# A transformer kernel on one core: down products of the last feed-forward with the activations stationary and 512 weight columns moving

## What is computed

```python
h2 = rms_norm(x, g_mlp)
x = x + jnp.square(jax.nn.relu(h2 @ w_up)) @ w_down      # w_up: 2048 x 8192, w_down: 8192 x 2048
```

## Time and profile before

| | |
|---|---|
| median of 3 runs | 2577.26 us (2576.41 to 2577.57) |
| time of the profiled execution | 2577.26 us |
| its span in the profile | 2575.6 us |
| mean granted TensorE clock | 0.999 of 2.4 GHz |
| TensorE busy | 2543.1 us, 99% |
| VectorE, ScalarE busy | 69%, 50% |
| DMA | 463.63 MB, 180 GB/s on average |

### The profile page before, as it was taken

One profiled execution on the slowest core, in us unless ns is written; L12 is line 12 of the kernel. 1 busy time (PEld: TensorE's weight loads), 2 busy tenths in 40 slices (PEclk: granted clock), 3 DMA queues, 4 the chain that ended last, 5 costly groups with the idle time before them and its releaser, 6 DMA issues.

```text
span 2575.6 us, 44260 instructions
## 1 busy us (share of the span) xinstructions
PE 2543.1 (99%) x14648; PEld 2240.0 (87%) x14648; DVE 1782.5 (69%) x2958; ACT 1288.6 (50%) x2372; POOL 255.7 (10%) x298
## 2 busy tenths in 40 slices
PE   7999999999999999999999999999999999999999
PEld 6888888888888888889999988888888888888888
DVE  6787789866886788675555566667575665665664
ACT  6656555444444444556555554555454444444443
POOL 0000114311330233100000000001100000000000
PEclk9999999999999999999999999999999999999999
DMA  6454435655556555545555545556465555555554
GB/s 229 163 168 159 164 131 196 193 185 193 184 167 206 187 187 180 193 141 188 175 173 177 162 153 185 184 184 214 153 212 186 187 182 190 186 186 188 182 190 137
DMA packets 163928, 463.63 MB, mean 180 GB/s; under 512 B 18106, under 2 KB 37470, under 8 KB 163806
## 3 DMA queue, kind: packets, MB, share of 16 engines
q1 hardware_dynamic: 163134, 459.91, 54.2%
q0 software_dynamic: 672, 2.11, 0.3%
HBM read 459.81 MB, written 2.14 MB: 179 GB/s over the span
## 4 chain that ended last, share of the span: by engine, by line
PE 82%; DVE 9%; ACT 4%; issue 3%; DMA 1%; POOL 0%; DVEq 0%; SPq 0%; ACTq 0%; POOLq 0%
PE G L712 72%; PE SB L712 9%; DVE wlo L1421 3%; ACT y L1214 1%; PE MB L712 1%; ACT whi L1129 1%; DVE wlo L1414 1%; DVE y L1629 1%; DMA x<-in_xT 0%; ACT y L1221 0%; PE SB L1059 0%; DVE og L1712 0%; ACT whi L1120 0%; DVE y L1809 0%; ACT aS L1292 0%
## 5 line engine op out<-in xcount | busy, mean ns | idle before, releaser
L712 PE MATMUL G<-hS,whi 128*128 128x512 f32 x3712 | 1299.7, 398 | 16.6 <-DVE wlo L1421 14.9
L712 PE MATMUL G<-hS,wlo 128*128 128x256 f32 x3680 | 996.5, 281 | 0.9 <-DVE hS L1863 0.9
L1421 DVE TENSOR_TENSOR wlo<-raw,whi 128x1024 fp32r<-128x1024 f32 (+3 forms) x790 | 902.5, 1182 | 97.8 <-ACT whi L1129 83.1
L712 PEld LDWEIGHTS G<-hS,whi 128*128 128x128 f32 x3712 | 685.3, 188 | 169.1 <-DVE wlo L1421 14.0
L1129 ACT ACTIVATE whi<-raw 128x1024 fp32r<-128x1024 f32 (+3 forms) x790 | 752.9, 998 | 79.6 <-DMA raw<-in_mix 31.1
L712 PEld LDWEIGHTS G<-hS,wlo 128*128 128x128 f32 x3680 | 696.8, 189 | 21.5 <-DVE hS L1863 1.3
L712 PE MATMUL G<-aS,whi 128*128 128x512 f32 (+1 forms) x1952 | 677.2, 398 | 0.8 <-DVE og L1523 0.7
L1192 ACT ACTIVATE tmp<-G 128x256 f32<-128x256 f32 x370 | 141.2, 382 | 879.2 <-PE G L712 879.2
L712 PE MATMUL G<-aS,wlo 128*128 128x256 f32 x1928 | 519.2, 281 | 0.0
L712 PEld LDWEIGHTS G<-aS,whi 128*128 128x128 f32 x1952 | 356.9, 188 | 77.9 <-DVE og L1523 1.0
L712 PEld LDWEIGHTS G<-aS,wlo 128*128 128x128 f32 x1928 | 364.4, 189 | 13.4 <-DVE aS L1716 0.3
(11 more groups left out here) (187 smaller groups left out, 1900.6 us busy)
## 6 DMA issues: line engine op xcount, KB each, us to landing
raw<-in_up SPq DMA_DIRECT2D x304, 512.0 KB, 4.6
raw<-in_dn SPq DMA_DIRECT2D x160, 512.0 KB, 4.5
raw<-in_in SPq DMA_DIRECT2D x192, 256.0 KB, 3.3
raw<-in_in SPq DMA_DIRECT2D x64, 512.0 KB, 4.6
raw<-in_out SPq DMA_DIRECT2D x64, 512.0 KB, 4.5
raw<-in_dn SPq DMA_DIRECT2D x64, 448.0 KB, 3.9
raw<-in_mix SPq DMA_DIRECT2D x64, 384.0 KB, 3.1
raw<-in_mix SPq DMA_DIRECT2D x64, 320.0 KB, 3.3
```

Of the source, the lines that this page charges most:

```text
L712: return pe.matmul(o, w, m, start=start, stop=stop, skip_group_check=False)
L1421: dve.tensor_tensor(wlo[:, slot, a * P:b * P], raw[:, h0 % RAW_SLOTS, 0:(b - a) * P], whi[:, slot, a * P:b * P].bitcast(F32), ALU.subtract ...
```

## The change

All products of `dn2_0`, `dn2_1`, `dn2_2`, and those of the first three iterations of `dn2_3`, are computed in groups of four output tiles (512 features) at once. For each of the 16 blocks of the depth, and each half of 128 tokens, the 128 x 128 activations are stationary and 512 weight columns move: high x high, high x low (`wlo`), low x high, all three summed in one bank. The result has tokens on the partitions. VectorE takes the two banks of a group into `y` (copies them in `dn2_0`, adds afterwards), so that `y` holds the sum over the chunks. At the end it is turned back with 32 PE transposes into the bank `MB` and added to `x`: the last four tiles' sum over three chunks during `up2_3`, the others during `dn2_3`. The last four tiles of `dn2_3` are computed as before. Units hold 4 x 4 blocks in place of 16 blocks of one tile, so a load takes two rows of 2 KB per partition in place of one of 4 KB, and the splits write in another order. On TensorE, ScalarE and VectorE the `dn2` stages are written out in place of the hardware loop; SP writes out `dn2_3` alone. Left out below: the declarations of two semaphores (`back_mm`, `back_added`), the view `yT` of `y`, those loops, the index of `tmp_done`, and empty lines.

```diff
@@ -64,6 +64,7 @@
 W_SLOTS = 4
 UNIT = 16
 AHEAD = 3
+TOKENS = ("dn2_0", "dn2_1", "dn2_2", "dn2_3")
 WIDE = {"up1_0": 4, "up2_0": 3}
 TOGETHER = 11
@@ -145,6 +146,8 @@
         self.bank0 = (prev.bank0 + prev.nm * (1 if prev.nm % 2 and prev.iters == 1 else 0)) % 2 if prev else 0
         self.half = (blocks + 1) // 2
         self.pieces = 3 if name == "in2" else 2
+        self.copied = (prev.copied + (prev.iters * prev.nm if prev.name in TOKENS else 0)) if prev else 0
         self.pbase = prev.pbase + prev.iters * prev.units * prev.pieces if prev else 0
         self.rbase = prev.rbase + (0 if prev.name == "in2" else 2 * prev.iters * prev.units) if prev else 0
@@ -156,6 +159,10 @@
     def g(self, it, p):
         return it * self.nm + (self.gbase + p)
+    def t(self, it, p):
+        return self.g(it, p) - self.copied - (3 * self.nm if self.name == TOKENS[-1] else 0)
     def u(self, it, k):
         return it * self.units + (self.ubase + k)
@@ -283,6 +290,19 @@
             return (G, (SB[2], SB[3]))[g % 2][h]
+        def by_tokens(st, it):
+            return st.name in TOKENS and (st.name != TOKENS[-1] or it < 3)
+        def token_banks(it):
+            return (SB[2], SB[3]) if it % 2 == 0 else (SB[0], SB[4])
+        def group_weights(tensor, slot, half):
+            w = tensor[:, slot, :].rearrange("p (k m n) -> p k m n", k=4, m=4)
+            return w[:, :, 2 * half:2 * half + 2, :]
         def in2_scores(g):
             return SB[0] if g % 2 == 0 else SB[4]
@@ -602,8 +629,13 @@
                     if not (isinstance(it, int) and h < RAW_SLOTS):
                         sp.wait_ge(lo_done, h - (RAW_SLOTS - 1))
+                    src = dram[st.name]
+                    if by_tokens(st, it if isinstance(it, int) else 0):
+                        rows = src[bass.ds(it * 4 + 2 * half, 2)][:, :, 4 * k * P:4 * (k + 1) * P]
+                        sp.dma_start(raw[:, slot, 0:(b - a) * P].rearrange("p (r c) -> p r c", r=2),
+                                     rows.rearrange("r p c -> p r c")).then_inc(landed[slot], 16)
+                        continue
                     row = it * st.units + k
-                    src = dram[st.name]
                     src = src[row] if isinstance(row, int) else src[bass.ds(row, 1)].rearrange("a p c -> (a p) c")
                     sp.dma_start(raw[:, slot, 0:(b - a) * P], src[:, a * P:b * P]).then_inc(landed[slot], 16)
@@ -746,7 +778,57 @@
                             one.then_inc(unit_used, 1)
+            def token_group(st, it):
+                banks = token_banks(it)
+                if it >= 2:
+                    pe.wait_ge(ev_done, st.g(it - 2, 3) + 1)
+                for kk in range(KT):
+                    k, within = divmod(kk, 4)
+                    slot = (st.ubase + k) % W_SLOTS
+                    if within == 0:
+                        pe.wait_ge(lo_done, st.piece(it, k, 1) + 1)
+                    if it == 0:
+                        pe.wait_ge(a_ready, A_BASE["up" + st.name[2:]] + kk + 1)
+                    if st.name == TOKENS[-1] and it and kk in (6, 12):
+                        turn_back(it - 1, kk // 12)
+                    h_w, l_w = (w[:, slot, within * 4 * P:(within + 1) * 4 * P] for w in (whi, wlo))
+                    for half in range(2):
+                        bank = banks[half][:, :]
+                        x_h = hS[:, kk, half * P:(half + 1) * P]
+                        x_l = hS[:, kk, T + half * P:T + (half + 1) * P]
+                        one = mm(bank, x_h, h_w, kk == 0, False)
+                        mm(bank, x_h, l_w, False, False)
+                        end = mm(bank, x_l, h_w, False, kk == KT - 1)
+                        if half == 0 and within == 0:
+                            one.then_inc(unit_used, 1)
+                end.then_inc(mt_done, 4)
+            def turn_back(it, pair):
+                pe.wait_ge(ev_done, ST[TOKENS[-1] if it < 3 else TOKENS[-2]].g(it, 3) + 1)
+                if it == 3 and pair:
+                    pe.wait_ge(back_added, 1)
+                elif it < 3:
+                    pe.wait_ge(back_added, 2)
+                    if it or pair:
+                        pe.wait_ge(x_done, 4 * it + 2 * pair)
+                for m in range(2):
+                    for half in range(2):
+                        at = (it * 4 + 2 * pair + m) * P
+                        end = pe.transpose(MB[:, m * T + half * P:m * T + (half + 1) * P], yT[:, half, at:at + P], ident)
+                end.then_inc(back_mm, 1)
             def mtile(st, it, p, last):
+                if by_tokens(st, it):
+                    if p == 0:
+                        token_group(st, it)
+                    return
                 if is_wide(st, it) and p < WIDE[st.name]:
                     if p == 0:
                         wide_start(st)
@@ -780,6 +862,12 @@
                 if st.name == "out2" and isinstance(it, int) and it == 0 and p < 2:
                     f = ST["out2"].g(0, 0) - 2
+                if st.prev and st.prev.name in TOKENS and isinstance(it, int) and it == 0 and p < 2:
+                    f = st.prev.g(0, 0)
+                if st.name == TOKENS[-1] and p < 2:
+                    f = st.g(0, 0)
                 if is_wide(st, it):
                     f = st.g(0, 0)
@@ -797,6 +885,10 @@
                 spreads = st.name in NORM_IN and isinstance(it, int) and it == 0 and p == (3 if st.wide else 2)
                 for kk in range(a, b):
+                    if st.prev and st.prev.name == TOKENS[-2] and first and (p, kk) in ((1, 4), (2, 4)):
+                        turn_back(3, p - 1)
+                    if st.name == TOKENS[-1] and p == 0 and kk in (6, 12):
+                        turn_back(2, kk // 12)
                     if st.name == "pre" and p == 2 and kk == 8:
                         norm_sums(NORM_IN["pre"])
                     if st.name == "up1_0" and isinstance(it, int) and it == 1 and (p, kk) in ((0, 6), (0, 13)):
@@ -847,6 +939,9 @@
                 high = accumulator(st, it, p)[:, 0:T]
                 pe.wait_ge(ev_done, g - 1)
+                if st.name == last2:
+                    pe.wait_ge(x_done, 12)
                 def at(kk):
                     k, within = divmod(st.start[p] + kk, st.blocks)
@@ -1418,6 +1520,11 @@
                     h0 = st.rbase + 2 * k + half
                     a, b = (0, st.half) if half == 0 else (st.half, st.blocks)
                     dve.wait_ge(hi_done, st.piece(it, k, half) + 1)
+                    if by_tokens(st, it):
+                        dve.tensor_tensor(group_weights(wlo, slot, half),
+                                          raw[:, h0 % RAW_SLOTS, :].rearrange("p (m k n) -> p k m n", m=2, k=4),
+                                          group_weights(whi, slot, half).bitcast(F32), ALU.subtract).then_inc(lo_done, 1)
+                        continue
                     dve.tensor_tensor(wlo[:, slot, a * P:b * P], raw[:, h0 % RAW_SLOTS, 0:(b - a) * P],
                                       whi[:, slot, a * P:b * P].bitcast(F32), ALU.subtract).then_inc(lo_done, 1)
@@ -1471,6 +1578,17 @@
                     dve.wait_ge(mt_done, st.g(it, 1) + 1)
                     fill_mixed(EARLY_TILES[p])
+                if st.name == TOKENS[-1] and 0 < it < 3 and p >= 2:
+                    add_back(it - 1, p - 2)
+                if st.name == TOKENS[-1] and it == 3 and p == 0:
+                    add_back(2, 0)
+                    add_back(2, 1)
+                if st.prev and st.prev.name == TOKENS[-2] and isinstance(it, int) and it == 0 and p in (1, 2):
+                    add_back(3, p - 1)
+                if by_tokens(st, it):
+                    if p == 3:
+                        read_tokens(st, it)
+                    return
                 if apart(st, p, last):
                     read_apart(st, it, p)
                     return
@@ -1512,12 +1630,30 @@
                 dve.wait_ge(done, count)
                 dve.tensor_tensor(tile_of(dest, m), og[:, p % 2, :], high, ALU.add).then_inc(ev_done, 1)
+            def read_tokens(st, it):
+                dve.wait_ge(mt_done, st.g(it, 3) + 1)
+                for half in range(2):
+                    dest, bank = yT[:, half, it * 4 * P:(it + 1) * 4 * P], token_banks(it)[half][:, :]
+                    if st.name == TOKENS[0]:
+                        end = dve.tensor_copy(dest, bank)
+                    else:
+                        end = dve.tensor_tensor(dest, dest, bank, ALU.add)
+                end.then_inc(ev_done, 4)
+            def add_back(it, pair):
+                dve.wait_ge(back_mm, (2 * it + 2 if it < 3 else 0) + pair + 1)
+                dest = x[:, it * 4 + 2 * pair:it * 4 + 2 * pair + 2, :]
+                dve.tensor_tensor(dest, dest, MB[:, :].rearrange("p (m t) -> p m t", m=2), ALU.add).then_inc(
+                    *((x_done, 2) if it < 3 else (back_added, 1)))
             def read_out(st, it, p):
                 g = st.g(it, p)
```

## The result

The changed kernel takes 2566.73 us (median of 6 runs, 2564.73 to 2567.85) against 2576.21 us of the kernel before (6 runs, 2574.68 to 2577.57). The ratio is 0.9962, with a 95% interval of 0.9952 to 0.9973. That is 9.5 us less, where 2.4 us more had been forecast, and it lies 1.3 us under the range. Rival 1 had said 8.8 us less.

The account below looks back on a forecast made before the run. TensorE's own matmul pitch was taken to bound the kernel: -1.6 us (512-column matmuls) + 3.5 (transposes) + 0.5 (one wait) = +2.4 us on 2577.3, forecast 2579.7 us. The range was 2568 to 2584 us.

Parts of the forecast that it names:

- Rival 1: Matmuls of the 15 groups: overhead is constant per matmul, a 512 takes 0.2267 us; -8.8 us in all, chance 0.15.
- TensorE's pitch is all that counts: Last feed-forward: the chain of waits never leaves TensorE from 1877 to 2571 us; VectorE and ScalarE matter only if late.
- The pitch of 512 columns: Matmuls of the 15 groups: a 512 takes 0.2339 or 0.235 us, so six save next to nothing; -1.6 us.
- The transposes: New work on TensorE's path: 32 in eight calls of four, 0.44 us a call; +3.5 us.
- Rival 3: Transposes on TensorE: each is paid at its duration, 0.274 us, 8.8 us in all; 2585.0 us, chance 0.03.
- The sum's own range: Whole kernel: the summed terms were said to lie between +0.7 and +5 us, 2578 to 2582.3 us.
- The wait of 0.5 us: Second transpose call in the last iteration: TensorE waits once for VectorE; +0.5 us, between 0 and 1.5.
- Cover: VectorE's reads, strided splits and 2 KB loads stay hidden under TensorE; splits run three units (17 us) ahead; no cost.
- Rival 2: Every matmul of the 15 groups: a 512 behind a 512 takes 0.24 us; +10.4 us, 2587.7 us, chance 0.14.
- Rival 4: Weight loads become the bound if 512 KB in 2 KB pieces need over 9.0 us; 2610 us at 10 us, chance 0.03.
- Rival 5: Stationary loads limit TensorE in the groups, and two of eight go; 91 us less, 2490 us, chance 0.01.

Follow-up runs that it names:

- e2: Kernel before, but the low product of the dn2 stages also moves all 512 columns, so every matmul there has 512: 2675.76 us (one run).
- e1: Kernel before, with each tile's last block ordered high product first, so 512 and 256 alternate strictly: 2561.44 us (median of 7), ratio 0.9965.
- e8: Changed kernel with each of the 32 transposes issued twice: 2572.51 us (one run).
- e5: Kernel before, with each tile's 512-column high and 256-column low products issued in runs of eight: 2556.46 us (median of 5), ratio 0.9925.
- e3: Kernel before, but the low product of the dn2 stages moves 384 columns, so 512 and 384 take turns: 2636.61 us (one run).
- e4: Changed kernel, but the groups' middle product moves only 256 of its 512 columns, giving 512, 256, 512: 2521.47 us (one run).
- e9: The kernel of e1 run once more, unchanged: 2553.27 us (one run).
- e11: Changed kernel with the strict alternation of e1 in all stages of the old form: 2564.51 us (median of 6), ratio 0.9946.

## Why the prediction was wrong, point by point

- **That TensorE's pitch is all that counts** held. So did the count: 15 groups, 96 matmuls for 64 pairs, the same columns.
- **The pitch of 512 columns failed.** "So a 512 seems to carry more beyond its columns than a 256 or a 384, and six of them save next to nothing." It was taken from a 512 with 256s around it: once as what is left of a pair when a 256's pitch is subtracted, once from two 512s at a boundary, right behind two 256s. Both gave 0.234 to 0.235, and both have the same fault, so their agreement proved nothing. Among its like a 512 takes 0.2267 us (after, e2), 13.3 ns over its columns, as a 384 and a 256 do. The term was -12.8 us and not -1.6. It had been worked out as an end of the range and as rival 1, and given 0.15.
- What the -12.8 us consist of: 32 matmuls fewer in a group at 13.3 ns, 0.43 us; and 64 pairs that lose the 6.7 ns which the mixed stream costs (0.3533 against 0.3467 in e1), 0.43 us. Each is 6.4 us over 15 groups. The first half is rival 1's reason. The second was named by no rival: the pitch at the boundary of tiles was read as a property of the matmul, not of its neighbours. So rival 1's 8.8 us came close to the 9.5 measured, but its reason gives only half of the term.
- **The argument against rival 1** ("no pitch of a 512 in the rows is as low as 0.2267") was true and weak, since all of those rows had mixed neighbours. The rows that could decide, the 384s of in2 among their like, stood in the earlier trace rows and were kept out of the sum.
- **The transposes** held: 0.44 us a call, 3.5 us. Rival 3 is out (e8).
- **The sum's own range** does not follow from its terms, which run from -2.3 + 3.5 + 0 = +1.2 to -0.8 + 3.5 + 1.5 = +4.2, not from +0.7 to +5. The measured time lies under either.
- **The wait of 0.5 us** did not come. TensorE passes from the first call in the last iteration (2541.90) to the second (2544.43) in 2.09 us with twelve matmuls, which is no more than their pitch. VectorE's timeline in the changed kernel (start us, us, what):

```profile
2539.83 1.29 DVE L1641 TENSOR_TENSOR y<-y,SB 128x512 f32<-128x512 f32 x2 [1.20 <-PE SB L744]
2541.15 2.36 DVE L1528 TENSOR_TENSOR wlo<-raw,whi 128x1024 fp32r<-128x1024 f32 x2
2543.43 0.68 DVE L1648 TENSOR_TENSOR x<-x,MB 128x512 f32<-128x512 f32 x1
```

It began to read the banks at once when the group ended (2539.8) and was through at 2541.1, 1.3 us later and not 1.5 to 1.9. Its two splits took 2.36 us together and not 2.44, and followed without a gap, so they ended 3.7 us after the group and not 4.4. The addition that frees MB ended at 2544.1, 0.3 us before TensorE asked.
- **Cover** held: VectorE's reads, the strided splits and the 2 KB pieces cost nothing. Rivals 2, 4 and 5 are out: 0.24 us a matmul, late loads, and 91 us from two loads of eight were not seen. The busy share of loads, by which the Trainium skill ("Perfetto Trace Analysis", Identifying the Most-Contended Engine) judges headroom, moved by one point, from 87 to 86%.

## What to carry to other kernels

Take the pitch of an instruction from a run of its like, not from what it costs beside others, and above all not by subtracting one from a mixed pair; if only mixed rows exist, give the law that the pure runs show (here columns plus 13.3 ns, twice) at least an even chance. On a stream that TensorE bounds, the same columns cost less in fewer and equal matmuls: where 512s and 256s take turns, issue them in runs. That gained 20 us here without any new layout, more than the whole change, and with both the gains did not add up.

## What had not been expected of the hardware

- Matmuls of one size, each with its own stationary load, cost their columns at 2.4 GHz and 13.3 ns: 0.120 us for 256 (e5: sixteen in 2.08 us, the last of which lasts 0.28, so fifteen starts in 1.80), 0.1733 for 384, 0.2267 for 512 (after, e2). Mixed they cost more: 512 with 384 13 ns a pair (e3), two 512s and a 256 13 ns for the three (e4: 3 x 0.1955 against 0.5734), 512 with 256 6.7 ns a pair or nothing (e9, e1).
- The strict alternation of 512 and 256 has two paces, 0.3467 and 0.3533 us a pair, at the same granted clock, kept over hundreds of us within one execution and different from one execution to the next; one kernel spread over 22 us by it. The pace was seen to change at a pause (e9) and behind a run of equal 512s (e11). What decides which pace follows, and the mechanism of the cost of mixing, were not found.
